# A hybrid attention and gated-linear-attention step: norms moved from GpSimd to ScalarE, one rest to VectorE, the second merge's first tile by contraction blocks, the samples' masks first

## The reference

```python
def step(S, xs):                                   # per chunk of a head
    qd, kt, vv, bl = xs
    o_inter = jnp.einsum('bihd,bhdv->bihv', qd, S)
    S = jnp.exp(bl[:, 0])[..., None] * S + jnp.einsum('bjhd,bjhv->bhdv', kt, vv)
    return S, o_inter
...
o_g = o_gla * lax.rsqrt(jnp.mean(o_gla * o_gla, axis=-1, keepdims=True) + NORM_EPS)
o_g = (o_g.astype(x.dtype) * gla_g).reshape(B, T, GLA_VAL_WIDTH) * jax.nn.silu(z_b)
g_a, g_b = jnp.split(merge, 2, axis=-1)
mix = jax.nn.sigmoid(g_a) * (o_nsa @ w_ba) + jax.nn.sigmoid(g_b) * (o_g @ w_bb)
return x + mix @ w_out
```

## Time and profile before

| | us |
|---|---|
| timed runs | 1350.67, 1353.56, 1360.87 |
| median | 1353.56 |
| profiled execution, span from first to last instruction | 1354.8 |
| profiled execution, time of its own | not given on the page |
| busy: PE, DVE, ACT, POOL | 1298.8, 619.4, 621.8, 145.7 |
| first gated head to the first merge's end | about 1000 to 1156 |

### The profile page before, as it was taken

The page is one execution under the profiler, slowest core; times in us unless marked ns, Lnnn a source line. Parts: engine busy times, 40 slices in busy tenths (PEclk is TensorE's granted clock), DMA queues, the critical chain, the costliest instruction groups (busy, mean ns, idle before and its releaser), DMA issues.

```text
span 1354.8 us, 23612 instructions
## 1 busy us (share of the span) xinstructions
PE 1298.8 (96%) x9533; PEld 1170.1 (86%) x9533; DVE 619.4 (46%) x1387; ACT 621.8 (46%) x1072; POOL 145.7 (11%) x184
## 2 busy tenths in 40 slices
PE   5999998999999999999999999999988989999998
PEld 4999998999988889989888889888866779999876
DVE  6211145645834343433323333466578767453342
ACT  6211336542555536666556645665467542221121
POOL 2100001103300000000000300313010260000000
PEclk9999999999999999999999999999999999899999
DMA  7251453522422211122212221554345656452331
GB/s 207 63 171 42 120 149 103 147 69 61 79 69 59 64 59 60 48 79 64 65 59 79 60 59 52 172 168 147 101 155 197 245 180 193 136 157 64 109 121 59
DMA packets 156908, 145.27 MB, mean 107 GB/s; under 512 B 27360, under 2 KB 141360, under 8 KB 156736
## 3 DMA queue, kind: packets, MB, share of 16 engines
q1 hardware_dynamic: 154016, 135.33, 33.1%
q0 software_dynamic: 2784, 8.43, 2.1%
HBM read 105.88 MB, written 41.88 MB: 109 GB/s over the span
## 4 chain that ended last, share of the span: by engine, by line
PE 56%; ACT 2%; DVE 2%; issue 1%; SPq 0%; DMA 0%; another core or an unknown queue 0%; POOL 0%; DVEq 0%; ACTq 0%
PE ps L240 31%; PE ps L2536 7%; PE ps L1645 4%; PE ps L1679 4%; PE ps L1661 3%; PE ps L1694 1%; PE ps L2443 1%; PE ps L2411 1%; DVE S L2648 1%; PE ps L2447 1%; PE ps L1764 1%; PE ps L2544 1%; PE ps L2502 0%; DMA m_raw<-in_w_branch_a 0%; SPq L3012 0%
## 5 line engine op out<-in xcount | busy, mean ns | idle before, releaser
L240 PE MATMUL ps<-hH,wH 128*128 128x352 f32 (+1 forms) x1320 | 440.0, 333 | 5.8 <-DVE stg L375 3.0
L240 PE MATMUL ps<-hH,wL 128*128 128x352 f32 (+1 forms) x1320 | 425.3, 322 | 0.0
L240 PE MATMUL ps<-hL,wH 128*128 128x352 f32 (+1 forms) x1320 | 424.8, 322 | 0.0
L240 PEld LDWEIGHTS ps<-hH,wH 128*128 128x128 f32 (+1 forms) x1320 | 248.1, 188 | 32.9 <-issue 26.5
L240 PEld LDWEIGHTS ps<-hL,wH 128*128 128x128 f32 (+1 forms) x1320 | 249.1, 189 | 2.2 <-issue 1.9
L240 PEld LDWEIGHTS ps<-hH,wL 128*128 128x128 f32 (+1 forms) x1320 | 247.8, 188 | 0.3
L227 DVE TENSOR_TENSOR wL<-w_raw,wH 128x1024 fp32r<-128x1024 f32 (+1 forms) x70 | 87.8, 1254 | 132.8 <-ACT wH L219 132.7
L2002 DVE CUSTOM_DVE_ANT_0 sP<-ps,dist,stat 128x256 f32<-128x256 f32 (+3 forms) x116 | 58.6, 542 | 176.8 <-issue 108.2
L360 ACT ACTIVATE stg<-ps 128x352 f32<-128x352 f32 x132 | 61.1, 463 | 119.1 <-PE ps L240 117.3
L219 ACT ACTIVATE wH<-w_raw 128x1024 fp32r<-128x1024 f32 (+1 forms) x70 | 73.5, 1050 | 70.5 <-issue 39.5
L2199 ACT ACTIVATE pPT<-ps 128x512 f32<-128x512 f32 x74 | 44.1, 596 | 131.9 <-PE ps L1661 131.8
(11 more groups left out here) (391 smaller groups left out, 2035.1 us busy)
## 6 DMA issues: line engine op xcount, KB each, us to landing
w_raw<-in_w_in SPq DMA_DIRECT2D x61, 512.0 KB, 4.1
p_spill<-stg SPq DMA_DIRECT2D x132, 176.0 KB, 1.8
zt<-p_spill SPq DMA_DIRECT2D x24, 528.0 KB, 4.8
w_raw<-in_w_in SPq DMA_DIRECT2D x17, 256.0 KB, 3.8
gvT<-p_spill SPq DMA_DIRECT2D x8, 528.0 KB, 5.4
x_all<-in_x_prompt SPq DMA_DIRECT2D x8, 512.0 KB, 10.0
m_raw<-in_w_branch_b SPq DMA_DIRECT2D x8, 512.0 KB, 5.5
xr<-in_x_prompt SPq DMA_DIRECT2D x8, 512.0 KB, 3.5
```

Source lines behind the costliest of these rows:

```text
L240: mm = nc.tensor.matmul(ps[0:t.m, bank, 0:NF], w[:, c % 2, t.m * k:t.m * k + t.m], x[n][:, k, :], start=(k == 0 and i == 0), stop=(k == t. ...
```

## The change

- `core`: the state products of the first half no longer wait for DVE; the masked products wait for ATs, the updates for Km. DVE makes ATs first, then Km.
- The low part of NSA block 2 moves from POOL to DVE, beside that of block 3.
- The norms of heads 2 and 3 (counted from 0) move from POOL to ACT (`late_norm`), 8 copies each with a scale column, behind the ACT work of tiles 1 and 3.
- The first tile of the second merge goes by contraction blocks, each as soon as its ogL is there; the last two blocks come together.
- In the first head `exp_below(2)` moves from before the outputs to after output 2, and `log_above(2)` from after output 1 to after output 3.

```diff
--- before.py
+++ after.py
@@ -2465,7 +2465,6 @@
                                  start=True, stop=True).then_inc(sem("sA_done"), 1)
                 pe.wait_ge(sem("S0_loaded"), 16 * (h + 1))
                 pe.wait_ge(sem("go_copied"), ncore * h + PT - 1)
-                pe.wait_ge(sem("sA_ready"), h + 1)
                 for q in range(2):
                     c = slice(DV * q, DV * q + DV)
                     for x in range(4):
@@ -2473,12 +2472,15 @@
                         nc.tensor.matmul(ps[32 * x:32 * x + DS, 6, c], qd[i][:, SEQ + DS * b:SEQ + DS * b + DS],
                                          state_of(h)[:, b, :],
                                          start=True, stop=False)
+                    if q == 0:
+                        pe.wait_ge(sem("sA_ready"), 2 * h + 1)
                     for x in range(4):
                         b = 4 * q + x
                         mm = nc.tensor.matmul(ps[32 * x:32 * x + DS, 6, c], ATs[:, DS * b:DS * b + DS],
                                               vh[i][0:ST, PT, :], start=False, stop=True)
                 mm.then_inc(sem("go_done"), 1)
                 pe.wait_ge(sem("go_copied"), ncore * h + PT)
+                pe.wait_ge(sem("sA_ready"), 2 * h + 2)
                 for q in range(2):
                     for x in range(4):
                         rows = slice(32 * x, 32 * x + ST)
@@ -2492,9 +2494,12 @@
             def turn(p):
 
                 f, j = divmod(p, 3)
-                pe.wait_ge(sem("og_normed"), f // 2 + 1)
+                if f < 4:
+                    pe.wait_ge(sem("og_normed"), f // 2 + 1)
+                else:
+                    pe.wait_ge(sem("act_normed"), GH + PT * (f // 2 - 1))
                 if j == 2:
-                    pe.wait_ge(sem("sample_normed"), f // 2 + 1)
+                    pe.wait_ge(sem("act_normed"), f // 2 + 1)
                 if p >= 2:
                     pe.wait_ge(sem("og_cut"), p - 1)
                 for t in range(4 * j, min(4 * j + 4, TILES)):
@@ -2517,15 +2522,29 @@
                     for p in pieces[len(pieces) * n // 3:len(pieces) * (n + 1) // 3]:
                         turn(p)
 
-            pe.wait_ge(sem("o_low"), R - 1)
-            pe.wait_ge(sem("o_low_last"), 1)
+            pe.wait_ge(sem("o_low"), R - 2)
+            pe.wait_ge(sem("o_low_last"), 2)
             tile(0)
             pe.wait_ge(sem("go_copied"), ncore * GH)
             pe.wait_ge(sem("sS_ready"), DB * GH)
             for c in range(1, KT):
                 tile(c)
-            pe.wait_ge(sem("og_low"), KT)
-            for c in range(KT, 2 * KT):
+            def first_of_second():
+
+                pe.wait_ge(sem("m_w_low"), KT + 1)
+                pe.wait_ge(sem("f_out"), KT - 1)
+                xH, xL = thirds(ogH), thirds(ogL)
+                for k in range(KT):
+                    pe.wait_ge(sem("og_low"), k + 1)
+                    if k == KT - 2:
+                        continue
+                    k0 = k - 1 if k == KT - 1 else k
+                    for n in range(3):
+                        mm = mring.products(KT, n, 3 * (KT % 2) + n, xH, xL, k0, k + 1)
+                mm.then_inc(sem("m_f_done"), 1)
+
+            first_of_second()
+            for c in range(KT + 1, 2 * KT):
                 tile(c)
 
             def out_products(t, half, bank, ks):
@@ -2586,7 +2605,7 @@
                     .then_inc(sem("o_low"), 1)
 
             def normed(h):
-                pool.wait_ge(sem("g_rstd"), 1 if h + 1 < GH else 2)
+                pool.wait_ge(sem("g_rstd"), 1)
                 nc.gpsimd.tensor_tensor(ogv[:, 0:PT, h, :], ogv[:, 0:PT, h, :],
                                         grv[:, 0:PT, h].unsqueeze(2).to_broadcast([P, PT, DV]), ALU.mult)\
                     .then_inc(sem("og_normed"), 1)
@@ -2594,10 +2613,10 @@
             pool.wait_ge(sem("zaF_loaded"), 16)
             for r in range(R):
                 gated(r)
-            for r in range(R - 1):
+            for r in range(R - 2):
                 o_rest(r)
-            pool.wait_ge(sem("o_low_last"), 1)
-            for h in range(GH):
+            pool.wait_ge(sem("o_low_last"), 2)
+            for h in range(GH - 2):
                 normed(h)
 
             pool.wait_ge(sem("ogT_done"), 3 * KT)
@@ -2637,9 +2656,9 @@
 
             def sample(h):
                 dve.wait_ge(sem("sA_done"), h + 1)
-                link(tt(Km[:, :, :], ps[:, 3, 0:P].unsqueeze(1).to_broadcast([P, 2, P]),
-                        bmt[:, :].unsqueeze(2).to_broadcast([P, 2, P]), ALU.mult))
                 tt(ATs[:, :], ps[0:ST, 3, 2 * P:2 * P + ST], tris[:, :], ALU.mult).then_inc(sem("sA_ready"), 1)
+                tt(Km[:, :, :], ps[:, 3, 0:P].unsqueeze(1).to_broadcast([P, 2, P]),
+                   bmt[:, :].unsqueeze(2).to_broadcast([P, 2, P]), ALU.mult).then_inc(sem("sA_ready"), 1)
 
             def sample_states(h):
                 dve.wait_ge(sem("su_done"), h + 1)
@@ -2728,9 +2747,10 @@
                     sums(dve, h + 2)
                 if not next1:
                     mring.low(dve, 0)
-                    dve.wait_ge(sem("o_high"), R)
-                    tt(oL[:, R - 1, :], oF[:, R - 1, :], oH[:, R - 1, :].bitcast(F32), ALU.subtract)\
-                        .then_inc(sem("o_low_last"), 1)
+                    for r in range(R - 2, R):
+                        dve.wait_ge(sem("o_high"), r + 1)
+                        tt(oL[:, r, :], oF[:, r, :], oH[:, r, :].bitcast(F32), ALU.subtract)\
+                            .then_inc(sem("o_low_last"), 1)
                     mring.low(dve, 1)
                 if next1:
                     tail_sums(link, h + 1)
@@ -2871,6 +2891,13 @@
                 act.wait_ge(sem("oS_gated"), r + 1)
                 nc.scalar.activation(oH[:, r, :], oF[:, r, :], ACT.Copy).then_inc(sem("o_high"), 1)
 
+            def late_norm(h):
+
+                act.wait_ge(sem("g_rstd"), 1 if h + 1 < GH else 2)
+                for t in range(PT):
+                    nc.scalar.activation(ogv[:, t, h, :], ogv[:, t, h, :], ACT.Copy,
+                                         scale=grv[:, t, h:h + 1]).then_inc(sem("act_normed"), 1)
+
             def sample_output(h):
                 act.wait_ge(sem("go_done"), ncore * (h + 1))
                 if h == 0:
@@ -2889,7 +2916,6 @@
                     for p in range(1, NV):
                         turned(act, 0, p)
                     exps(act, 1)
-                    exp_below(act, 2)
                 else:
                     if next1:
                         exps(act, h + 1)
@@ -2901,7 +2927,9 @@
                         turned(act, h + 1, t)
                     if h == 1 and t == 1:
                         exp_below(act, 3)
-                    if next2 and t == 1 + 2 * h:
+                    if h == 0 and t == 2:
+                        exp_below(act, 2)
+                    if next2 and t == 3:
                         log_above(act, h + 2)
                     if not next1 and t == 1:
                         sd(0)
@@ -2925,13 +2953,15 @@
             act.wait_ge(sem("g_rstd"), 3)
             for h in range(GH):
                 nc.scalar.activation(ogv[0:ST, PT, h, :], ogv[0:ST, PT, h, :], ACT.Copy,
-                                     scale=grv[0:ST, PT, h:h + 1]).then_inc(sem("sample_normed"), 1)
+                                     scale=grv[0:ST, PT, h:h + 1]).then_inc(sem("act_normed"), 1)
 
             for c in range(KT):
                 for f in turns[c]:
                     act.wait_ge(sem("og_cut"), 3 * f + 3)
                     nc.scalar.activation(ogH[:, f, :], z_of("zb", f)[:, :], ACT.Copy).then_inc(sem("og_high"), 1)
                 mring.high(act, c + 2)
+                if c in (1, 3):
+                    late_norm(2 if c == 1 else 3)
             for f in range(KT):
                 if f + 2 < KT:
                     mring.high(act, KT + f + 2)
```

## The result

The changed kernel takes 1343.8 us (median of 7 runs, 1341.98 to 1347.57), against 1353.56 us before; the ratio is 0.9922, with a 95% interval of 0.9904 to 0.9941. The forecast was 1343.3. The 0.78% of difference is small, but the interval leaves out 1. The profiled execution has a time of 1343.8 us and a span of 1342.1, so 1.7 us lie around the span.

What follows compares the result with a forecast made beforehand. PE, busy 96% of the span, was taken as the bound, so only its waits and slow clock pay. 0.3 + 0.83 + 1.09 + 2.74 + 5.3 = 10.3 us off the median 1353.56 gave 1343.3 us; range 1337 to 1352.

Steps and rivals of the forecast that it cites:

- Step 1: Samples' stage of head 3: the first state products start without the masks, so PE's whole wait of 0.83 us goes.
- Step 2: Heads 1 and 2: masks gain 0, as PE then waits longer for DVE; moving Exp and Ln gains 0.3 us.
- Step 3: First merge's start: low part 0 no longer meets POOL's third subtraction; 1.09 us gained, head 4's 0.83 included.
- Step 4: Third transpose: with two norms off POOL, low part 2 meets nothing; the stall shrinks from 3.29 to 0.55, 2.74 us gained.
- Step 5: Second merge's first tile by blocks: the 2.69 us wait for ogL and the low clock's 2.6 go, together 5.3.
- Rival A: The wait at low part 2 is the DMA's, so 1.6 us are lost: 1345.0 us, or 1346; chance 0.12.
- D: Second merge's first tile: changing PSUM bank every 3 matmuls is dearer, 9.4 us lost, 1352.7 us; chance 0.04.
- F: POOL's norms or DVE's order still block DVE; only masks and blocks work: 7.5 us gained, 1346.1 us; chance 0.07.
- E: Heads: the clock falls at the longer wait of 1.25 us, costing 29 us less the 10.3 gained, 1372 us; chance 0.05.
- B: Second merge: the clock is not part of the gain, so the sum without 2.6 is 7.7 us, 1345.9; chance 0.16.
- C: Before's median run also had a clock dip after the 3.29 us stall: 12.9 us gained, 1340.7; chance 0.14.

Runs made afterwards that it cites:

- o1_order: The kernel before with only the moves of Exp and Ln in the first head; ratio 0.9998 (0.9984 to 1.0013).
- m1_masks: The kernel before with only the samples' masks part of the change; ratio 0.9948 (0.9932 to 0.9965), 7 us less.
- t1_tails: The changed kernel with DVE's products for the next head's tails ahead of the samples' masks, heads 1 to 3; 1341.27 us beside 1344.13, ratio 0.9897.
- p1_poollate: The changed kernel with POOL's second norm started only behind PE's second transpose, across DVE's low part 2; ratio 0.9933 (0.9910 to 0.9955).
- b1_blocks: The kernel before with only the second merge's first tile by contraction blocks; ratio 0.9954 (0.9938 to 0.9969), 6.2 us less.
- r1_rest: The kernel before with only the second subtraction moved to DVE; ratio 0.9994 (0.9984 to 1.0003).
- k1_warm: The kernel before with 14 spare PE matmuls in the 2.69 us wait for the last ogL; ratio 0.9982 (0.9968 to 0.9996), 2.4 us less.

## Why the prediction was right

By its own steps, with the measured marks:

| step | forecast | measured |
|---|---|---|
| 2: heads 1 and 2 | 0.3 | 0.39 (45.84 to 45.45) |
| 1: head 3 | 0.83 | 1.02 |
| 3: head 4 and first merge | 1.09 | 1.04 |
| 4: stall at the third transpose | 2.74 | 3.17 |
| 5: wait and low clock | 5.3 | 5.39 (2.76 + 2.63) |
| sum | 10.3 | 11.0 |

The remaining 1.7 us between the spans lie ahead of the first head, where both kernels are the same.

*Step 1* was under-sized. I took the bracket (0.83), which counts from the modelled end of L2464; from start to start L2473 followed L2464 by 1.05 us before, 1088.28 to 1089.33, and by 0.04 after, 1085.20 to 1085.24. That difference is the 1.02, to 0.01 us. The row of before in PE's timeline:

```profile
1088.28 0.22 PE L2464 MATMUL ps<-qd,ki 128*32 128x32 f32 x2
```

*Step 2* was right for a partly wrong reason: the moves of Exp and Ln give 0.10 (o1_order), the masks 0.16 in the first head and 0.14 in the second (m1_masks), where I had 0.3 and 0. The rest of the masks' 0.83 is lost there, as said; t1_tails shows the cause by giving it back.

*Step 3* held: 0.69 us for low part 0, 2.42 for both oL.

*Step 4* held in its cause (p1_poollate) and was 0.4 us short: the samples' copy comes 2.4 us earlier and not 1.66, by the same mis-sized 0.83, twice, and the heads' 0.39 that I had left out. So ACT's conversion starts at 93.55 behind the first L2443 instead of 96.22, and no stall is left. But the forecast gave this gain to the norms' part alone, while m1_masks loses the stall without it. The gain of the five parts alone (4.6, 2.7, 3.2, 1.1 and 0.2 us without the clock) sums to 11.8; together they give 8.4, because masks and norms remove the same stall.

*Step 5* held in the profile, and its size was partly chance. Of 13 waits of 2.7 to 3.3 us that the profiles above show at these two places, 11 were followed by a low clock, of 1.5 to 1.6 us in nine and 2.6 to 2.7 in two. Before's profile had one of the two long ones, and one of the two waits without any. The timed runs point the same way. Each lists its mean granted clock: over the 58 runs of before that stand beside the experiments the middle value is 0.993, over the 13 of the changed kernel 0.996, while before's profile has 0.995. So a usual execution of before has more low clock than its profile, about twice 1.5 us by the waits above (an estimate), 3.0 for the 2.6 that I subtracted.

*The time* of 1343.3 came closer than the sum that gave it, and that was luck. Without the clock the sum had 7.7 us, and 8.4 were measured; with 3.0 us of clock that makes 11.4 where I had 10.3. Over 20 runs of before and six of the changed kernel taken together the medians are indeed 1355.88 and 1344.13, 11.8 us apart. But I started from 1353.56, the median of three runs and also of the result's seven, and the medians of the three later sets of before (15, 20 and 23 runs) lie 2.3 to 2.5 us above it. The low start and the short sum cancelled.

Rival A is refuted by p1_poollate, D by the steps of 0.16 us in the changed kernel and b1_blocks, F by low parts of 0.69 us. E did not happen: none of the 14 waits of 1.3 us in the heads, two in each of the seven profiles that have them, was followed by a low clock. B and C each hold something: the low clock can miss a wait (B) and usually follows the first stall too (C). What stays open is why the low level lasts 1.5 us' worth in one execution and 2.7 in another.

## What to carry to other kernels

Read a long row beside the other engine's: the DVE operations here that took several times their usual length all ended within about half a microsecond behind a POOL instruction, and their price was what was left of it, which any shift of the schedule changes. Moving that one instruction (p1_poollate) tells whether it is the cause. So measure parts alone and together: here a change of two masks removed a stall of 3.3 us at quite another place. A wait of PE of about 3 us usually cost half as much again in clock here (11 of 13); spare matmuls show that share by themselves, and contraction blocks in the order in which they become ready remove both.

## What the runs showed of the hardware

- POOL's multiplication over SBUF held up DVE's subtractions with both inputs in SBUF (3.53, 3.64, 3.78 us for 0.69), and even scalings of 128x8 and 32x4 elements in SBUF (3.23 for 0.47 and 2.07 for 0.15, r1_rest). I had not expected the tiny ones. Two other kinds ran beside it at their usual length: DVE's state updates, which read PSUM (eight in 3.21 us beside the first norm, before and after, and in 3.22 with POOL idle), and the reciprocals of the same small tile, 0.20 and 0.17 us, that ran while a norm was under way in r1_rest.
- DVE gets in between two POOL instructions that follow each other (m1_masks), and then POOL is the one that waits: the four norms took 15.21 instead of 14.76 us.
- The granted clock fell to 0.50 behind a wait of only 0.83 us once in 24 (b1_blocks, first head), amid the samples' small matmuls, and cost 1.05 us, while a wait of 3.3 us left it at 1.00 in two profiles (before, k1_warm).
- ACT's copy with a scale column over 128 x 256 elements in place takes 0.41 us from start to start (3.29 for eight), the same as over 32 partitions.
